# Order of work in the even mixer, form and place of the modulation products, and turning of their rows

## The reference

```
for layer in 0, 1:
    mods = silu(cond) @ ada_w[layer] + ada_b[layer]      # 2 condition rows, 9 x 1024 columns
    x = ffn_sublayer(x, mods 0..2)                       # swiglu, d_ff 2816, then layer norm
    h = modulate(x, mods 3..4)
    o = even_mixer(h) (layer 0) or odd_mixer(h) (layer 1)
    x = deepnorm_residual(x, mods 5 * o)
    x = ffn_sublayer(x, mods 6..8)
```

## Time and profile before

| | |
|---|---|
| runs | 3044.34 us median of 3 (3043.14 to 3049.86) |
| profiled execution | 3042.88 us, span 3041.1 us |
| busy in the span | PE 94%, PEld 79%, DVE 50%, ACT 43%, POOL 23% |
| mean granted TensorE clock | 0.961 of full |
| DMA | 352.88 MB, 116 GB/s mean |
| even mixer, projections to scan | from about 442 to 959 us of the span |
| feed-forward part before and after it | about 40 to 430, and 1075 to 1500 us |

### The profile page before, as it was taken

The page is one execution under the profiler, slowest core; times in us unless marked ns, Lnnn a source line. Parts: engine busy times, 40 slices in busy tenths (PEclk is TensorE's granted clock), DMA queues, the critical chain, the costliest instruction groups (busy, mean ns, idle before and its releaser), DMA issues.

```text
span 3041.1 us, 44000 instructions
## 1 busy us (share of the span) xinstructions
PE 2864.1 (94%) x17352; PEld 2394.9 (79%) x17352; DVE 1523.9 (50%) x2614; ACT 1317.8 (43%) x2452; POOL 687.1 (23%) x624
## 2 busy tenths in 40 slices
PE   8999988999998899999899998889979999899998
PEld 6888876866676678888688886879979888898778
DVE  5443348447722644433533334565553555535666
ACT  4443336411112444433433334555544476444673
POOL 1111120021112410111211112111124533545324
PEclk9999999999988999999999997899989999999999
DMA  6442312233322145432222321224533433444334
GB/s 251 152 148 97 102 65 67 93 118 107 118 84 83 56 146 166 153 104 97 67 97 96 102 97 63 77 91 156 185 120 131 141 123 118 139 139 132 121 102 139
DMA packets 97437, 352.88 MB, mean 116 GB/s; under 512 B 10704, under 2 KB 12880, under 8 KB 96848
## 3 DMA queue, kind: packets, MB, share of 16 engines
q1 hardware_dynamic: 97232, 350.07, 35.0%
HBM read 348.97 MB, written 1.05 MB: 115 GB/s over the span
## 4 chain that ended last, share of the span: by engine, by line
PE 74%; DVE 10%; ACT 7%; issue 5%; POOL 2%; DMA 1%; SPq 0%; DVEq 0%; ACTq 0%; POOLq 0%
PE ps L1453 19%; PE ps L1455 18%; PE ps L1454 18%; PE ps L1484 4%; ACT spl L1752 2%; DVE spl L1964 1%; PE ps L1492 1%; PE ps L1508 1%; DVE work L2129 1%; PE ps L1476 1%; PE ps L1477 1%; PE ps L1706 1%; POOL bigr L2393 1%; DVE work L2047 1%; ACT big L1907 1%
## 5 line engine op out<-in xcount | busy, mean ns | idle before, releaser
L1453 PE MATMUL ps<-bigr,spl 128*128 128x256 f32 (+1 forms) x3880 | 1342.2, 346 | 74.7 <-issue 21.2
L1454 PE MATMUL ps<-bigr,spl 128*128 128x256 f32 (+1 forms) x3880 | 1312.9, 338 | 0.0
L1455 PE MATMUL ps<-bigr,spl 128*128 128x256 f32 (+1 forms) x3880 | 1312.9, 338 | 0.0
L1964 DVE TENSOR_TENSOR spl<-ring,spl 128x512 fp32r<-128x512 f32 x954 | 759.9, 813 | 889.9 <-ACT spl L1752 885.3
L1752 ACT ACTIVATE spl<-ring 128x512 fp32r<-128x512 f32 x1140 | 687.7, 625 | 780.0 <-PE ps L1455 728.7
L1453 PEld LDWEIGHTS ps<-bigr,spl 128*128 128x128 f32 x3880 | 749.7, 193 | 190.7 <-issue 45.2
L1454 PEld LDWEIGHTS ps<-bigr,spl 128*128 128x128 f32 x3880 | 751.6, 194 | 76.3 <-issue 2.2
L1455 PEld LDWEIGHTS ps<-bigr,spl 128*128 128x128 f32 x3880 | 750.1, 193 | 76.3
L2393 POOL TENSOR_TENSOR bigr<-work,bigr 128x512 fp32r<-128x512 f32 (+1 forms) x200 | 210.1, 1056 | 1079.6 <-ACT bigr L1756 1079.4
L2388 POOL TENSOR_TENSOR spl<-ring,spl 128x512 fp32r<-128x512 f32 x186 | 253.8, 1366 | 361.8 <-ACT spl L1752 361.6
L1756 ACT ACTIVATE bigr<-work 128x512 fp32r<-128x512 f32 (+2 forms) x232 | 120.6, 522 | 279.2 <-DVE work L2024 127.6
(11 more groups left out here) (278 smaller groups left out, 2596.8 us busy)
## 6 DMA issues: line engine op xcount, KB each, us to landing
ring<-w_stream SPq DMA_DIRECT2D x640, 512.0 KB, 3.3
big<-w_stream SPq DMA_DIRECT2D x16, 512.0 KB, 10.9
X<-x_t SPq DMA_DIRECT2D x2, 1024.0 KB, 14.0
cst<-consts SPq DMA_DIRECT2D x1, 1601.5 KB, 7.2
X<-mem_t SPq DMA_DIRECT2D x1, 1024.0 KB, 5.8
out_t<-X SPq DMA_DIRECT2D x8, 128.0 KB, 2.1
prm<-params SPq DMA_DIRECT2D x1, 249.5 KB, 2.8
```

The lines of the kernel that those rows point to most:

```text
L1453: pe.matmul(out, hi, x[0], start=k == 0, stop=False)
L1454: pe.matmul(out, hi, x[1], start=False, stop=False)
L1455: finish(pe.matmul(out, lo, x[0], start=False, stop=k == nk - 1), tile, key if k == nk - 1 else None)
L1964: dve.tensor_tensor(lo_half(h), raw_half(h), hi_half(h), SUB).then_inc(*sig("lo", h, by="lo_dve"))
```

## The change

1. All 14 remaining groups of layer 0 are done split, in the first feed-forward part (`ada(0, range(4, 18))`, 112 advances). Four groups of layer 1 are done unsplit in the scan of the even mixer (16 advances). The other 14 groups of layer 1 are done split in the second feed-forward part (112 advances).
2. In the even mixer there are no pumps any more outside the scan; in the scan one stands after `scan_v` and one at the end of a step.
3. The conformer's taps are advanced singly (124 `cstep`), channel tiles 0 and 1 first, then 2 and 3. Their places: 27 in the projections, 4 in the turns, 7 in `prep(0)`, 4 in each of the 20 levels, 3 in `ending(3)`, the last 3 in steps 0 and 1 of the scan. `conformer_norm` begins in scan step 2.
4. The projections alternate: one of q, k, v and then half a glu pair or one z; `l2norm` follows one unit later.
5. Rows are turned by fours: the rows of up to four groups go to partitions 0, 32, 64 and 96 of one `arow` (the condition is placed at an offset in its zeroed tile), and one `ada_turn` with K = 128 turns them; DVE adds the bias for each group. 11 turns stand in place of 36. The start zeroes `arow` and larger condition tiles.
6. `pos["pool"]` is not set in the even mixer any more (no split was planned there while it was on). `NCH` is 659 in place of 656.

```diff
@@ def ada
+                for i in range(0, len(groups), 4):
+                    gs = groups[i:i + 4]
                     row, rfree, ri = arows.get()
+                    for j, g in enumerate(gs):
...
+                            yield "ada_raw" if raw else "ada", l, g, k, j, bank, free, tile
+                            if k == 1 and prev:
+                                yield from turn(*prev)
...
+                        yield "ada_row", l, g, j, row, bank, rfree
+                        if j == len(gs) - 1:
+                            prev = gs, row, ri
@@ def conformer
-                for j in range(1, 31):
-                    for m in range(4):
-                        yield "conformer", j, m
-                        if m % 2:
+                for p in (0, 2):
+                    for j in range(31):
+                        for m in (p, p + 1):
+                            yield "conformer", j, m
                             yield CUT
@@ def even_mixer
+                for n, m in enumerate((0, 4, 1, 5, 2, 6, 3, 7, 8, 9, 10, 11)):
+                    yield from qkv(m, first if n == 0 else None)
+                    if normed:
+                        yield from l2norm(normed.pop(0))
+                    if m < 8:
+                        normed.append(m)
+                    if n >= 8:
+                        yield from z_of(n - 8)
+                    elif n % 2 == 0:
+                        half = yield from glu_of(n // 2)
+                    else:
+                        yield from half()
+                    if len(padded) > 1:
+                        yield from cstep(3)
@@ turns, prep(0), levels, ending(3)
-                    yield from pump()
+                        if t % 2:
+                            yield from cstep()
-                        yield from pump()
+                        yield from cstep()
...
                         yield from advance(side)
-                        yield from pump()
                         yield from cstep()
                         for d in range(2):
                             b, free, bi = banks.get()
                             yield "level_u", h, d, lv, b, free
+                            if d == 0:
+                                yield from cstep()
                         yield from advance(side)
-                        yield from pump()
                         yield from cstep(2)
...
-                        yield from pump(2)
+                        yield from cstep()
@@ scan
+                pos["unsplit"] = True
...
+                    yield from pump()
                     kt, ki = keys
...
-                    yield from pump(2)
+                    if s < 2:
+                        yield from cstep(2)
...
+                    yield from pump()
@@ order
-            gens.append(ada(0, range(4, 10)))
+            gens.append(ada(0, range(4, 18)))
             xs, ms = yield from ffn(0, T, xs, ms, ("ln_g00", "ln_b00"), ("ln_g00", "ln_b00", 0, 3, 4))
-            gens.append(ada(0, range(10, 18)))
             gens.append(ada(1, range(18)))
-            pos["unsplit"] = True
             xs, ms = yield from even_mixer(xs, ms)
@@ tensor ada_turn
-                w.wait_ge(*done("ada_row", l, g))
+                w.wait_ge(*done("ada_row", l, gs[-1]))
                 for q in range(4):
-                    ins = pe.matmul(bank[:, 2 * q:2 * q + 2], row[:, q * 128:(q + 1) * 128], P("sel4")[0:4, :], start=True, stop=True)
+                    ins = pe.matmul(bank[:, 8 * q:8 * q + 8], row[:, q * 128:(q + 1) * 128], P("sel8"), start=True, stop=True)
@@ vector start
+                dve.memset(arow[:, :], 0.0).then_inc(*sig("arow_0"))
+                dve.memset(csr[:, :].bitcast(F32), 0.0).then_inc(*sig("csr_0"))
                 dve.memset(c4[:, :], 0.0).then_inc(*sig("cond_0"))
```

More of the change, by code:

```diff
@@ L24 @@
 HC = CH // 2
-NCH = 656
+NCH = 659
 NEG = -1.0e30
@@ L42, in add, with turn_sel @@
         out.append((name, n, fn))
-    add("sel4", 2, lambda a: np.concatenate([np.eye(2), np.eye(2), np.zeros((124, 2))]).astype(np.float32))
+    def turn_sel(a):
+        v = np.zeros((128, 8), np.float32)
+        for j in range(4):
+            for r in range(4):
+                v[32 * j + r, 2 * j + r % 2] = 1
+        return v
+    add("sel8", 8, turn_sel)
     add("cond", 16, lambda a: np.stack([cols(a["c"][0]), cols(a["c_ctx"])], -1).reshape(128, 16))
@@ L514, in ada, with turn @@
             def ada(l, groups):
+                groups = list(groups)
                 prev = None
-                def turn(g, row, ri):
+                def turn(gs, row, ri):
                     bank, free, bi = banks.get()
[L519 to L532, removed]
-                    row, rfree, ri = arows.get()
[L534 to L537, removed]
@@ new lines, in turn @@
+                    yield "ada_turn", l, gs, row, bank, free
+                    arows.give(ri, ("ada_t", l, gs[0]))
+                    banks.give(bi, ("mod", l, gs[-1]))
+                for i in range(0, len(groups), 4):
+                    gs = groups[i:i + 4]
+                    row, rfree, ri = arows.get()
+                    for j, g in enumerate(gs):
+                        bank, free, bi = banks.get()
+                        for k in range(KD):
+                            raw = k % 2 == 0 if pos["unsplit"] == "half" else pos["unsplit"]
+                            tile = yield from take([("ada_w", (l,), 128 * k, 128, 512 * g, 512, 0)], 512, raw)
+                            yield "ada_raw" if raw else "ada", l, g, k, j, bank, free, tile
+                            if k == 1 and prev:
+                                yield from turn(*prev)
+                                prev = None
+                            if k < KD - 1 and (k % 2 or not raw):
+                                yield CUT
+                        yield "ada_row", l, g, j, row, bank, rfree
+                        banks.give(bi, ("ada_row", l, g))
+                        if j == len(gs) - 1:
+                            prev = gs, row, ri
+                        yield CUT
@@ L711, in even_mixer, with cstep, qkv @@
                 chain_ = gate_chain()
-                for m in range(12):
-                    b, bi = first if m == 0 else (yield from linear(("qkv_mm", m), tile_of("even_w_in", (0,), 128 * m), src, T))
+                cgen, padded = conformer(), set()
+                def cstep(n=1):
+                    for _ in range(n):
+                        yield from advance(cgen)
+                def qkv(m, r=None):
+                    b, bi = r or (yield from linear(("qkv_mm", m), tile_of("even_w_in", (0,), 128 * m), src, T))
                     cp, free, ci = CP.get()
@@ L735, in even_mixer @@
                     banks.give(bi, ("sz", m))
-                cgen = conformer()
-                def cstep(n=1):
-                    for _ in range(n):
-                        yield from advance(cgen)
+                half, normed = None, []
+                for n, m in enumerate((0, 4, 1, 5, 2, 6, 3, 7, 8, 9, 10, 11)):
[12 more added lines that the diff above has]
+                        yield from cstep(3)
+                yield from flush()
                 b, free, bi = banks.get()
@@ L888, in even_mixer @@
                         yield s
+                pos["unsplit"] = False
                 fm = [("so", 7, 1)]
```

82 lines of the change are left out of this document (44 added, 38 removed).

## The result

The changed kernel takes 2997.95 us, median of four runs (2996.49 to 2999.68), beside 3045.2 us (3043.14 to 3049.86) for the kernel before on the same chip: a ratio of 0.9843, 95% interval 0.9826 to 0.986. It is 47 us faster; 43 were forecast, and the forecast time was 3001. The profiled execution took 2999.68 us, its span 2997.9 us.

A forecast was written before the change was run, and what follows sets the result against it. PE's work plus its waits was taken as the bound. Terms +43.3 (feed-forward), -12 (turns, `prep(0)`), -48.6 (levels), -12 (`ending(3)`), -10 (projections), -4 (scan) sum to -43.3: 3001 us, range 2978 to 3031 at 0.8.

The forecast's parts named there:

- What bounds the kernel: Whole kernel: PE's work plus its waits, PE busy 94% of the span; in the levels PE's own work sets the pace.
- The feed-forward term: Both feed-forward parts: moved split steps at 0.45 us each, 28.8 and 20.7 us, less 6.2 us for turns: +43.3 us.
- The rule weighed: Levels: by weight loads PE is used 62% only, so removing 87 us could bring little more than 18; decided against.
- Levels: Levels: DVE becomes the bound, a level takes 6.1 to 6.6 us, 134 us in all: -48.6, bounds -68 and -30.
- Projections: Projections: alternating with glu and z halves DVE's load for each product: -10 us, bounds -16 and +20.
- The rival of the taps: Projections: taps ahead of L1964 in DVE's queue hold up the splits, +20 in place of -10: 3031 us; chance 0.12.
- Turns, `prep(0)` and `ending(3)`: Turns with `prep(0)`: -12 us, bounds 8 to 15 off; `ending(3)`: -12 us, bounds -9 and -13; unsplit advances leave both.
- a rival with the levels: From `prep(0)` to `ending(3)`: the clock stays at half, small matmuls there double: 3069 us; chance 0.08.
- Scan: Scan: keeps its products, loses three row turns and one more behind it: -4 us; the pump after `scan_v` nothing.
- The rival of the clock: Levels: PE's clock sags, half of the stretch granted at 1.2 GHz, 28 us more: 3029 us; chance 0.15.
- the mark that the prediction had set for it: Levels: a granted clock below 0.9 was to show the prediction wrong.

The follow-up runs named there:

- small taps: Changed kernel with the taps from `prep(0)` to `ending(3)`, except tap 0, computing 2 columns of 512: 2964.01 us, ratio 0.9737.
- pairs: Changed kernel with each level's four taps two ahead of the first `level_u`, none between the two, two after: 2986.49 us, ratio 0.9814.
- idle products: Changed kernel with 40 unread fp32 products of 256 columns in the levels, one in each half level: 2999.37 us, ratio 0.9855.
- single steps: Changed kernel with unsplit modulation put back one step at a time: 6 in `prep(0)`, 35 in the levels, 6 in `ending(3)`: 2978.68 us, ratio 0.9785.
- the kernel with 25 advances: Changed kernel with 25 unsplit modulation advances put back: 3 in `prep(0)`, 19 in the levels, 3 in `ending(3)`: 2982.48 us, ratio 0.98.

## Why the prediction was right, and where it was not

**What bounds the kernel.** Right. The feed-forward stretches are full and unsplit work bound the levels: with it in place PE is busy 164 of 168 us, without it DVE sets the pace, and with small taps PE is again the busiest, 90 of 99 us.

**The feed-forward term** was forecast to the microsecond, +43.3 against +43.7 by stage, from one pace (50 / 223) and two counts. It rests on the pace being the same with and without modulation mixed in, and 50.00 of 50 us after shows that it still is. The forecast left out that the start loses two turns as well: the first tile product begins 0.9 us earlier for it, and the feed-forward part gave that back.

**The rule weighed.** By weight loads the levels could have given little more than 18 us. They gave 56, with the order's help, and 34 with the old order and DVE's work as it was; and the busy time of loads fell from 114 to 88 us. The runs decide against that reading for a stage of unsplit 512-column products. It was the prediction's own reading: the Trainium skill, page "Trainium Kernel Development and Optimization", section "Performance Expectations", speaks of how close a kernel is to roofline, and names MFU (the share of the peak arithmetic rate that the products use) beside the weight loads.

**Levels**: the mechanism right, the term mis-sized: "a level comes to 6.1 to 6.6 us" was 6.3, but "with a few waits for POOL in `prep` I take 134 us" added 8 us too much. The 0.755 us for a tap was also not what it did: by the same division, busy time by count, it is 62.2 / 75 = 0.83. The mean of one went from 0.809 to 0.849.

**Projections** (-5.6 against -10). The gain is the alternation (6.7 us by the old order put back), and the bound of +20 for taps holding up splits was wide: taking them all out gives 0.9 us. The rival of the taps falls. The step that was mis-sized is "most of the 7.4 us of idle time there". In the projections before, PE waited three times for a split of DVE, 2.56, 4.53 and 2.08 us; one such wait is left, 5.01 us behind a short conv, and it stands in the kernel with no taps in the projections too. The longest before and the one after (start, us, engine, instruction, idle time before):

```profile
473.33 0.79 PE L1453 MATMUL ps<-bigr,spl 128*128 128x512 f32 x1 [4.53 <-DVE spl L1964]
...
502.08 0.79 PE L1491 MATMUL ps<-bigr,spl 128*128 128x512 f32 x1 [5.01 <-DVE spl L2008]
```

**Turns, `prep(0)` and `ending(3)`** came 2 us short each (-9.9, -9.7, inside their bounds). Both ran at a lower clock, 0.77 and 0.70, and the small matmuls of `ending(3)` at half: the forecast put that into a rival with the levels and left it out of these two terms. With three unsplit advances back in `prep(0)` the clock was 1.00, and turns and `prep(0)` took 18.8 us in place of 21.0, with more work on PE.

**Scan** (-0.4 against -3): its three turns are gone, but its first products ran at half clock. And the pump behind `scan_v`, which the forecast put at nothing, fills 2 us of gaps. The timeline of the kernel after, from `ending(3)` into the scan (start, us, engine, instruction, idle time before):

```profile
790.27 2.77 PE L1668 MATMUL ps<-big 64*64 64x128 f32 x32 [2.82 <-DVE big L2262]
...
792.97 3.68 PE L1678 MATMUL ps<-work,big 64*128 64x64 f32 x32
...
797.36 1.97 PE L1688 MATMUL ps<-big 128*64 128x128 f32 x8 [0.71 <-POOL big L2486]
799.26 1.97 PE L1694 MATMUL ps<-big 128*128 128x64 f32 x8
...
813.67 1.09 PE L1688 MATMUL ps<-big 128*64 128x128 f32 x8
...
833.98 5.51 PE L1557 MATMUL ps<-cst,big 128*128 128x1 f32 x32
839.35 3.55 PE L1562 MATMUL ps<-cst,work 128*128 128x1 f32 x16
```

Eight records of L1688 take 1.97 us at the start of the scan and 1.09 later, and the key products take 3.68 us where the earlier trace rows has 2.00. Windows of 5 us of the same scan:

```profile
797.40:802.40 5.00, 5.00 (x22) 4.55 (x23) 1.41 (x3) 0.00 (x0) 2.67 (x3) 0.50 0.00 0
802.40:807.40 5.00, 5.00 (x15) 3.21 (x14) 0.69 (x1) 0.00 (x0) 0.00 (x0) 0.50 0.00 0
...
812.40:817.40 5.00, 5.00 (x34) 3.59 (x32) 4.02 (x6) 0.00 (x0) 0.94 (x1) 1.00 0.30 105
...
837.40:842.40 5.00, 5.00 (x25) 5.00 (x25) 0.00 (x0) 0.00 (x0) 0.00 (x0) 0.50 0.00 0
```

The clock is at half for the first 10 us, behind an `ending(3)` in which PE waited for DVE, and again at 837, where PE does the single-column sums of the conformer's norm. That second sag stands in each of the scans looked at, before and after; the first is in the changed kernel and in those with single turns, with the old order of the projections and with both pumps at the end of a step. It is not in the one with pairs, whose `ending(3)` ran at 0.81. But neither is it in the one with no taps in the projections nor in the modulation's move alone, whose `ending(3)` ran at 0.61 and 0.63: so a slow `ending(3)` with waits of PE isn't enough for it, and its cause stays open.

**The rival of the clock** happened in a small size. The clock in the levels was 0.90, just at the mark that the prediction had set for it, but DVE set the pace, and 0.97 with idle products gave nothing in all. "What kept it full beside small matmuls was always an unsplit product" doesn't hold for these kernels: with small taps the levels ran at 1.00 with no unsplit product in them. The Trainium skill, page "TensorE: Matmul & The Clock Gate", section "HAM oscillation — how this bites in real kernels", says of bursts of matmuls with long waits between them that each starts at the throttled clock. The start of the changed kernel's scan agrees (1.97 us against 1.09), the scans that begin at full clock behind an `ending(3)` at 0.61 and 0.63 don't, and the levels do only in part, since 0.90 and not 0.50 was granted.

**The total is right by luck.** Projections, turns, `ending(3)`, scan, the layer norm and the feed-forward parts gave 13 us less than forecast, and the levels, the way to the second column sum and the untouched rest 13 us more. That the sum comes out within 0.1 us is chance.

**The parts don't add up as it had them.** It took each edit as a term of its own. With turns by fours and everything else old: 3012.0 us. The new order as well: 3000.9 (-11). The modulation moved as well: 2998.0 (-3). But the move alone on the kernel before costs 9 us. It would be easy to say that the move pays only where 40 taps leave the levels, and the levels do gain 9 us more from it then (182.6 to 148.9, against 168.4 to 126.1). But from column sum to column sum the mixer is 57.3 us shorter both times: the scan took 3.3 us less in the one and 6.0 more in the other, where its clock was 0.87 in place of 0.93. What differs is the price. The feed-forward parts are 69.2 us longer in the old kernel and 58.2 in the new. With the move come 14 turns there and 4 here, and ten turns at 1.04 us are the difference. So by the stage sums it is the turns by fours, and not the order of work, that tell the +9 from the -3; and the -3 is smaller than the 4.4 us by which the untouched rest differs. The move on top of turns by fours in the old order wasn't run.

**What stays open.** Why pairs of taps let the levels run 5.3 us faster is seen only in DVE's shorter idle time; which tap's place does it wasn't tried. The scan's 6.9 us come with the clock, and whether its start can be kept at full clock on purpose wasn't found. The scan took 100.4 to 101.3 us where its clock was 0.93 (pairs, single steps, the modulation left in place), 107.3 and 108.2 at 0.87, 111.7 at 0.84; but the kernel with 25 advances had its `ending(3)` at a clock of 1.00 and a scan of 108.2 all the same, by longer sags around the sums. The pairs together with the 25 advances weren't run. The part behind the second feed-forward part, untouched by any edit, took 1574 to 1580 us in the profiled executions; so the 2.9 us of the table's last row can't be put down to the change. Nor is it known why the way from the scan to the second column sum takes 75 to 76 us in some of these kernels and 78 to 84 in others.

## What to carry to other kernels

When work is taken off the bounding engine in a stage, the stage falls only to what the next engine needs there: 66 us less on PE bought 34 with DVE at 140 us, and 64 less bought 42 once 40 taps had left DVE's queue. Then ask what the work costs where it goes: both moves made the mixer 57.3 us shorter, and the one cost 69 us in the feed-forward parts and the other 58. Work that fits into the gaps of the former bound should stay: 38 steps in the levels cost 5.6 us, and would cost 17 in the feed-forward part at 0.45 each. Small matmuls such as turns are paid by their count in a stage that PE bounds, so gathering them gave 28 us in the stages, 31 in all, without a change of schedule.

## What was not expected of the hardware

- A tap takes 0.66 to 0.74 us alone and up to 1.78 beside an addition of POOL. The timeline of the kernel after:

```profile
723.05 0.74 DVE L2198 SCALAR_TENSOR_TENSOR big<-big,prm 128x512 f32<-128x512 f32 x1
...
724.69 1.26 POOL L2481 TENSOR_TENSOR big<-big 128x512 f32<-128x512 f32 x1
724.72 1.78 DVE L2198 SCALAR_TENSOR_TENSOR big<-big,prm 128x512 f32<-128x512 f32 x1
```

The first tap runs alone; the second begins with POOL's addition and ends 0.55 us after it. Of the 77 taps in the levels the 51 that meet no record of POOL take 0.73 us on the average, and the 26 that meet one 1.05. Over the levels this is about 26 x 0.32 = 8 us of DVE, an estimate from the two means, and DVE is the bound there. The Trainium skill, page "SBUF — State Buffer", section "SBUF: two separate sides", says that a DVE instruction with two inputs from SBUF and one of POOL that reads SBUF lock each other out of a shared pair of ports, and that the one which starts first has it for its whole length. This pair agrees, since the tap ends 0.55 us after POOL, not far from a tap's own time. So does the other case: at 726.76 the taps begin first, and the addition of POOL at 726.83 takes 1.79 us in place of 1.26.

- Under the single-column sums of the conformer's norm the clock falls to half although PE is recorded busy 5.00 of 5 us, and what follows pays: the unsplit pair behind them takes 3.50 us at 842.76 in place of 1.94 at 828.79. This happens in the kernel before too.
- A start of the scan at half clock costs several of its 107 us with the same instructions: the scans of 635 to 637 PE records that begin at full clock took 100.4 to 104.3. That is more than some edits here are worth. A difference of a few us between two orders of work is read only after the clock of each stage.
